# Order of the three matmuls of a split float32 product, and where the low half of the weights lies in its 256-byte line

## The reference

```python
h = h + 0.5 * swiglu(rmsnorm(h, ffn1_norm[l]), ffn1_w_gate[l], ffn1_w_up[l], ffn1_w_down[l])
h = h + hybrid_mixer_2(rmsnorm(h, mix_norm[l]), w_in[l], w_attn_out[l], ...)
h = h + 0.5 * swiglu(rmsnorm(h, ffn2_norm[l]), ffn2_w_gate[l], ffn2_w_up[l], ffn2_w_down[l])
```

## Time and profile before

| | |
|---|---|
| median of 3 runs | 1447.43 us (1447.2 to 1447.82) |
| profiled execution | 1447.49 us |
| its span in the profile | 1445.7 us |
| TensorE matmul busy | 1437.9 us (99%), 11649 matmuls |
| weight loads busy | 1412.6 us (98%), beside the matmuls |
| VectorE, ScalarE, GpSimd busy | 898.3, 770.2, 496.2 us |
| mean rate of the DMA queues | 174 GB/s |

### The profile page before, as it was taken

One profiled execution on the slowest core, in us unless ns is written; L12 is line 12 of the kernel. 1 busy time (PEld: TensorE's weight loads), 2 busy tenths in 40 slices (PEclk: granted clock), 3 DMA queues, 4 the chain that ended last, 5 costly groups with the idle time before them and its releaser, 6 DMA issues.

```text
span 1445.7 us, 31241 instructions
## 1 busy us (share of the span) xinstructions
PE 1437.9 (99%) x11649; PEld 1412.6 (98%) x11649; DVE 898.3 (62%) x1568; ACT 770.2 (53%) x1113; POOL 496.2 (34%) x213
## 2 busy tenths in 40 slices
PE   9999999999999999999999999999999999999998
PEld 8899999999999999999999999999999999999987
DVE  6438888745445469989644434444447998864433
ACT  6556565555445446567544544444545567655443
POOL 6550000543334303710244442433420570044442
PEclk9999999999999999999999999999999999999999
DMA  7434566645556545445565654555644545567663
GB/s 268 134 110 160 177 193 190 218 163 163 177 176 213 169 134 164 143 162 161 178 176 176 208 182 134 184 174 187 202 157 140 174 133 180 170 201 205 206 193 111
DMA packets 74779, 250.94 MB, mean 174 GB/s; under 512 B 15824, under 2 KB 16848, under 8 KB 74704
## 3 DMA queue, kind: packets, MB, share of 16 engines
q1 hardware_dynamic: 74416, 249.38, 55.3%
q10 hardware_dynamic: 288, 0.54, 0.1%
HBM read 247.79 MB, written 1.05 MB: 172 GB/s over the span
## 4 chain that ended last, share of the span: by engine, by line
PE 98%; DVE 1%; ACT 1%; issue 0%; DVEq 0%; ACTq 0%
PE W L1784 28%; PE W L1786 28%; PE W L1785 28%; PE XP L1925 2%; PE XQ L1925 2%; PE W L1879 1%; PE W L1841 1%; PE W L1878 1%; PE W L1877 1%; PE W L1843 1%; PE W L1842 1%; PE XQ L2038 0%; PE XP L1930 0%; DVE scr L1429 0%; PE XP L1879 0%
## 5 line engine op out<-in xcount | busy, mean ns | idle before, releaser
L538 POOL TENSOR_TENSOR wlo<-raw,whi 128x1024 fp32r<-128x1024 f32 (+1 forms) x185 | 475.7, 2576 | 899.6 <-ACT whi L618 899.1
L1784 PE MATMUL W<-xh,whi 128*128 128x272 f32 (+2 forms) x2400 | 688.8, 287 | 0.1
L1786 PE MATMUL W<-xh,wlo 128*128 128x272 f32 (+2 forms) x2400 | 685.7, 286 | 0.0
L1785 PE MATMUL W<-xl,whi 128*128 128x272 f32 (+2 forms) x2400 | 679.9, 283 | 0.0
L618 ACT ACTIVATE whi<-raw 128x1024 fp32r<-128x1024 f32 (+1 forms) x440 | 480.9, 1099 | 110.4 <-PE W L1786 71.3
L1784 PEld LDWEIGHTS W<-xh,whi 128*128 128x128 f32 x2400 | 451.6, 188 | 2.5 <-issue 1.5
L1786 PEld LDWEIGHTS W<-xh,wlo 128*128 128x128 f32 x2400 | 453.0, 189 | 0.0
L1785 PEld LDWEIGHTS W<-xl,whi 128*128 128x128 f32 x2400 | 451.7, 188 | 0.2
L1111 DVE TENSOR_TENSOR wlo<-raw,whi 128x1024 fp32r<-128x1024 f32 (+1 forms) x255 | 331.7, 1301 | 80.0 <-ACT whi L618 79.5
L1784 PE MATMUL W<-ax,whi 128*128 128x272 f32 (+2 forms) x992 | 282.9, 285 | 0.6 <-DVE ax L1550 0.4
L1785 PE MATMUL W<-ax,whi 128*128 128x272 f32 (+2 forms) x992 | 282.2, 284 | 0.0
(11 more groups left out here) (287 smaller groups left out, 1216.7 us busy)
## 6 DMA issues: line engine op xcount, KB each, us to landing
raw<-in_w SPq DMA_DIRECT2D x377, 512.0 KB, 3.6
raw<-in_w SPq DMA_DIRECT2D x64, 704.0 KB, 4.0
proj<-proj SPq DMA_DIRECT2D x16, 64.0 KB, 3.9
scr<-in_cst SPq DMA_DIRECT2D x1, 1000.0 KB, 8.0
h<-in_hT SPq DMA_DIRECT2D x3, 272.0 KB, 4.4
raw<-in_w SPq DMA_DIRECT2D x2, 256.0 KB, 3.8
proj<-in_gain SPq DMA_DIRECT2D x1, 512.0 KB, 4.6
out<-proj SPq DMA_DIRECT2D x4, 128.0 KB, 1.8
```

Of the source, the lines that this page charges most:

```text
L538: pool.tensor_tensor(low(j, place), packed(j, place), high(j, place).bitcast(F32), ALU.subtract).then_inc(lo_ready[j], 1)
L1784: pe.matmul(out, wh, mh, start=start and k == 0, stop=False, skip_group_check=True)
L1785: pe.matmul(out, wh, ml, start=False, stop=False, skip_group_check=True)
L1786: ins = pe.matmul(out, wl, mh, start=False, stop=stop and k == len(pairs) - 1, skip_group_check=True)
```

## The change

In every group of three matmuls over slabs, the one with the low weights moves from the last place to the first: low weights by high activations, then high by high, then high by low. The flags that open and close an accumulation, and the semaphore's increment, move with the first and last place. The functions that do this are `slab`, `first_pair`, `first_slab` and `second_slab`; `last_down` keeps its order.

In `x_place` and `a_places` the low part is placed one row further back: chunk k of the low weights now starts 16 (or 26) floats further in its line than the stream of chunk k-1. In `t_places` the low part moves by 32 floats. `d_places` is unchanged.

```diff
-TOKEN_BEHIND = (0, 0)
+TOKEN_BEHIND = (0, LINE // 2)
...
 def x_place(t, j):
-    return Place(DC, P, P + T % LINE, column(X_AT + t, WHI_AT, j, X_BEHIND[t]), column(X_AT + t, WLO_AT, j, X_BEHIND[t]))
+    return Place(DC, P, P + T % LINE, column(X_AT + t, WHI_AT, j, X_BEHIND[t]), column(X_AT + t - T, WLO_AT, j, X_BEHIND[t]))
...
-    return tuple(Place(DC, P, P + ROW % LINE, column(X_AT + t, WHI_AT, j, high), column(X_AT + t, WLO_AT, j, low))
+    return tuple(Place(DC, P, P + ROW % LINE, column(X_AT + t, WHI_AT, j, high), column(X_AT + t - ROW, WLO_AT, j, low))
...
-                    pe.matmul(out, wh, mh, start=start and k == 0, stop=False, skip_group_check=True)
-                    pe.matmul(out, wh, ml, start=False, stop=False, skip_group_check=True)
-                    ins = pe.matmul(out, wl, mh, start=False, stop=stop and k == len(pairs) - 1,
+                    pe.matmul(out, wl, mh, start=start and k == 0, stop=False, skip_group_check=True)
+                    pe.matmul(out, wh, mh, start=False, stop=False, skip_group_check=True)
+                    ins = pe.matmul(out, wh, ml, start=False, stop=stop and k == len(pairs) - 1,
                                     skip_group_check=True)
...
-                        pe.matmul(out, wh, mh, start=k == 0, stop=False, skip_group_check=True)
-                        pe.matmul(out, wh, ml, start=False, stop=False, skip_group_check=True)
-                        ins = pe.matmul(out, wl, mh, start=False, stop=k == DC - 1, skip_group_check=True)
+                        pe.matmul(out, wl, mh, start=k == 0, stop=False, skip_group_check=True)
+                        pe.matmul(out, wh, mh, start=False, stop=False, skip_group_check=True)
+                        ins = pe.matmul(out, wh, ml, start=False, stop=k == DC - 1, skip_group_check=True)
```

More of the change, by code:

```diff
@@ L1958, in first_slab @@
                     wh, wl = weights(0, first_x(0)[0], k)
-                    pe.matmul(out, wh, xh[:, k, :], start=k == 0, stop=False, skip_group_check=True)
-                    pe.matmul(out, wh, xl[:, k, :], start=False, stop=False, skip_group_check=True)
-                    ins = pe.matmul(out, wl, xh[:, k, :], start=False, stop=k == DC - 1, skip_group_check=True)
+                    pe.matmul(out, wl, xh[:, k, :], start=k == 0, stop=False, skip_group_check=True)
+                    pe.matmul(out, wh, xh[:, k, :], start=False, stop=False, skip_group_check=True)
+                    ins = pe.matmul(out, wh, xl[:, k, :], start=False, stop=k == DC - 1, skip_group_check=True)
                     if k == 2:
@@ L1976, in second_slab @@
                         wh, wl = weights(1, first_x(1)[1], k)
-                        pe.matmul(W[1][:, 0:T], wh, xh[:, k, :], start=k == 0, stop=False, skip_group_check=True)
-                        pe.matmul(W[1][:, 0:T], wh, xl[:, k, :], start=False, stop=False, skip_group_check=True)
-                        ins = pe.matmul(W[1][:, 0:T], wl, xh[:, k, :], start=False, stop=k == DC - 1, skip_group_check=True)
+                        pe.matmul(W[1][:, 0:T], wl, xh[:, k, :], start=k == 0, stop=False, skip_group_check=True)
+                        pe.matmul(W[1][:, 0:T], wh, xh[:, k, :], start=False, stop=False, skip_group_check=True)
+                        ins = pe.matmul(W[1][:, 0:T], wh, xl[:, k, :], start=False, stop=k == DC - 1, skip_group_check=True)
                 ins.then_inc(mm_done, 1)
```

## The result

| | before | after |
|---|---|---|
| median | 1447.72 us (15 runs, 1447.2 to 1448.31) | 1450.51 us (15 runs, 1449.76 to 1450.98) |
| profiled execution, span | 1447.49, 1445.7 us | 1450.36, 1448.6 us |

The ratio is 1.0018, 95% interval 1.0011 to 1.0025. The changed kernel is 2.8 us slower; the forecast was 7.3 us faster, and its range did not hold the time.

A forecast was written before the change was run, and what follows sets the result against it. The prediction took the distance between TensorE's matmul starts as the bound. Its terms, 3.3 + 0.5 + 1.4 + 0.6 + 1.1 + 0.4 = 7.3 us, off 1447.49 us gave 1440.2 us, range 1431 to 1447.6.

The forecast's parts named there:

- What bounds the kernel: TensorE, busy 1437.9 of 1445.7 us: time is the number of matmuls times the distance between their starts.
- The step that failed: Slabs over `xh` and `ax`: 2 to 3 ns per chunk whose third load lies 16 floats too far; equal offsets remove it.
- The ladder of three offsets: Third-load offsets 16, 32, 48 take 2.965, 2.982, 3.0025 us per 24 matmuls at 272 tokens; same order at 256.
- `xh`, 272: Slabs over `xh` with 272 tokens: 186 slabs gain 17.6 ns each, 3.3 us.
- `xh`, 256 outside the first block: Slabs over `xh` with 256 tokens: 62 slabs gain 23 ns each, 1.4 us.
- `ax` in slabs of 8: 14 slabs with 272 tokens gain 37.5 ns each, 0.5 us; 14 with 256 gain 44 ns each, 0.6 us.
- First block: Its up slabs gain 22 ns each, 1.1 us; 8 slabs of 258 over `ax` gain two steps each, 0.4 us.
- First pairs and down slabs: Interleaved first pairs: 0, bound 0.3 us either way; down slabs: offsets stay 16, so 0.
- Last down projection: Offsets 0, 0 and 32 become 0, 0 and 0; nothing gained, bounds -0.2 to +0.2 us.
- The first: Rival: down slabs differ in more than the third offset, so nothing changes, 1447.4 us; chance 0.15.
- The second rival: Equal offsets let 256-wide and 258-wide slabs fall into the fast rate, 2.735 us per 24 at 256; 1431.2 us; chance 0.13.
- The third: Rival: low load's tail meets the next row at offset 0, costing 4.7 ns per chunk; 1453.6 us; chance 0.10.

The follow-up runs named there:

- experiment 1: Changed kernel's order with every place as before the change; 1447.67 us, ratio to before 0.9999.
- experiment 3: Changed kernel with low part over `xh` 0, 16, 32, 48 floats back by slot; 272 tokens: 2.980, 3.027, 3.000, 3.020 us per slab.
- experiment 5: Changed kernel with low part over `xh` at its old place for 272 tokens, 32 floats back for 256 and 258; 1449.85 us, ratio 1.0014.
- experiment 10: Changed kernel, low part by slot -8, 8, 24, 40 back at 272 (3.001, 2.993, 2.975, 3.011 us per slab), 32, 32, 32, 16 at 256.
- experiment 12: Kernel with old places at 272 (1442.9 us), over `xh` high part 4 back at 272, low 32, 32, 32, 16 back at 256; 1447.56 us, ratio 1.0002.
- experiment 9: Changed kernel with the low part at its old place wherever 272 tokens stream; 1442.90 us, ratio 0.9967.
- experiment 6: Changed kernel with three 272-token up projections streaming 256, 264 or 240 columns; 2.760, 2.929, 2.680 us per slab.
- experiment 11: Changed kernel, 272: high part -8, 8, 4, -4 back by slot, low old: 3.045, 3.026, 2.964, 3.025 us per slab; 256: low 24 back, 2.822.

## Why the prediction was wrong

**What bounds the kernel** was right. TensorE's distance between starts is the time, the waits did not grow, and the order by itself cost nothing; experiment 1 shows it to 0.1 us in every stage.

**The step that failed** is the one that read a rule out of rows 3 to 8: "a cost of 2 to 3 ns for each chunk whose third load lies 16 floats too far", and with it "every load is then at the offset of the down slabs", so that all slabs would go at their rate. The ladder of three offsets was real, but it compared slabs that differ in row pitch and in how the load lies against the following row as well. With the high part held still, the border load's offsets of 32, 16, 0 and 48 gave 2.980, 3.027, 3.000 and 3.020 us at 272 (the first two in uniform kernels as well, the last two in one slot of four only): not a ladder, and the value 16 at its bad end. The rows had a sign of this: the earlier trace rows show 256 tokens over `xh` with the same places, at 2.805 us and, between slabs of 258, at 2.84. Term by term:
- `xh`, 272: forecast -3.3 us, measured +7.4. This term alone turns the sign.
- `xh`, 256 outside the first block: forecast -1.4, measured -3.0. Right in direction, but the forecast had half the size, and the direction was luck: the slabs got 2.760, where other places and stages give 2.733 to 2.893 us.
- `ax` in slabs of 8: forecast -0.5 and -0.6 for 272 and 256, measured +0.1 and 0.0. Their first offset did change, from 48 to 16; it brought nothing.
- First block: forecast -1.1 and -0.4, measured -1.3 and -0.3. The sum was right by luck: 22 ns were forecast for each of 52 slabs over `xh`, and the 21 of 256 gained 58 ns each, the 31 of 258 only 5.
- First pairs and down slabs: forecast 0, measured 0.0 and +0.1. Very first slabs: forecast nothing, measured +0.3. Last down projection: forecast 0 within 0.2, measured -0.3.

**The rivals.** The first (the offset is no cause) is refuted in that places do move the rate: in one order, uniform kernels took 2.982 and 3.027 us at 272 tokens and differed in the low part's place alone. Its doubt, though, was the right one, and I gave it too little weight: the 94 ns between the down slabs of the earlier trace rows had equal offsets. I took odd and even rows for the reason. In the changed kernel, whose down slabs have the same places, the timeline of slabs 1 to 3 of that stage reads:
```profile
263.28 0.28 PE L1785 MATMUL W<-ax,wlo 128*128 128x256 f32 x1
...
267.17 0.28 PE L1785 MATMUL W<-ax,wlo 128*128 128x256 f32 x1
...
270.94 0.28 PE L1785 MATMUL W<-ax,wlo 128*128 128x256 f32 x1
...
274.83 0.28 PE L1785 MATMUL W<-ax,wlo 128*128 128x256 f32 x1
```
Slab 1 (odd rows) takes 3.89 us, slab 2 (even rows) 3.77, slab 3 3.89: before it was the odd slab that took 3.76. Experiment 1, in the order of the changed kernel and with the same down slabs, has the fast odd slab again (starts of slabs 1 to 3 at 264.29, 268.05 and 271.95 us). So neither the rows nor the order set it; what is left is the state in which the stage is entered.

The second rival, a fast string at 2.735 us for 256 tokens, exists (2.733 in experiments 3, 5, 10 and 12), but equal offsets are not what leads to it: the changed kernel has them and took 2.760, and with the border load at 0 instead of 16 the slabs went at 2.733 or at 2.893 by stage. The third, the load's tail against the next row at a price that decides from 3.6 ns per chunk on, was nearest at 272, and its sign came true (slabs over `xh` above 2.99, down slabs unchanged): they lost (3.027 - 2.982) / 8 = 5.6 ns per chunk, gain and price together. At 256 the same tail came with a gain of 5.6 ns, so as a rule it fails too. Which part of a load collides with which part of a stream was not measured, and no run separates the head of a load from its tail; the runs show only that the width of the stream, the places of both parts and the state at entry all enter. Nor did a run take away what the other engines and the DMA read and write meanwhile. Against their amount as the cause stand the two projections of experiment 12, the same loop at two rates; a part of theirs in the timing is not excluded.

The Trainium skill (TensorE: Matmul & The Clock Gate, "Step-by-step: what each phase is for") says that loading the next weights takes no read bandwidth from the running matmul. By it all the runs from 1442.9 to 1453.9 us that compute the same would have one time. Here the measurement decides: with equal matmuls, widths and order, 24 of them take from 2.733 to 2.893 us by where weights lie and by the state at entry. Whether read bandwidth is what they lack, no run shows.

## What to carry to other kernels

Where TensorE streams without a pause and reloads weights for every matmul, the distance between starts depends on where weights lie against the rows that stream, and on the state in which a slab is entered, by up to 6% here. (All places here are counted within lines of 256 bytes; that this is the period that matters was not tested.) It is no sum of costs per load, so a rate seen in one arrangement may not be carried to another width, to other neighbours or to another stage. Sweep the places on the chip, with all slots set as they will run, choose them separately for each width, and change only the stages in which the rate was seen. And when rows with equal parameters show two rates, as the down slabs did, do not build on their mean: find out first what the two are.

## What the runs showed of the hardware that was not expected

- The same loop with the same places runs at 3.000 or 3.053 us per slab from one projection to the next, at the granted clock of 2.4 GHz, and keeps its rate through 36 slabs (experiment 12). With 256 columns: 2.733 or 2.893, in experiment 5 and in experiment 12 within one execution each, and in the opposite stages.
- The rates repeat to the nanosecond from stage to stage and from kernel to kernel (2.982 us at 272 in experiments 5 and 9 as before, 2.760 at 256 in the changed kernel and in experiments 6 and 9). They look like locked patterns and not like noise.
- The high part moved by 4 floats (16 bytes) in all slots changed slabs of 272 from 2.982 us (experiment 9) to 3.000 or 3.053 (experiment 12), while one slot of four moved alike had gone down to 2.964 (experiment 11).
